# The scan's old state added on VectorE's two diagonal blocks, in place of a unit-matrix product and a mask

## The reference, cut to what matters

```
def step(S, inp):
    r_t, w_t, k_t, v_t, aa_t, bb_t = inp
    sa = jnp.einsum('bhvk,bhk->bhv', S, aa_t)
    S = S * w_t[:, :, None, :] + sa[..., None] * bb_t[:, :, None, :] + v_t[..., None] * k_t[:, :, None, :]
    y_t = jnp.einsum('bhvk,bhk->bhv', S, r_t)
    return S, y_t
```

## Time and profile before

| what | value |
|---|---|
| median of 3 runs | 1130.45 us (1130.41 to 1130.87) |
| profiled execution | 1130.62 us |
| its span in the trace | 1129.0 us |
| PE busy | 1093.8 us (97% of the span) |
| DVE busy | 689.9 us (61%) |
| granted TensorE clock | 0.997 of full speed |

### The profile page before, as it was taken

The page is one execution under the profiler, slowest core; times in us unless marked ns, Lnnn a source line. Parts: engine busy times, 40 slices in busy tenths (PEclk is TensorE's granted clock), DMA queues, the critical chain, the costliest instruction groups (busy, mean ns, idle before and its releaser), DMA issues.

```text
span 1129.0 us, 18123 instructions
## 1 busy us (share of the span) xinstructions
PE 1093.8 (97%) x6736; PEld 862.5 (76%) x6736; DVE 689.9 (61%) x1167; ACT 506.0 (45%) x910; POOL 92.9 (8%) x145
## 2 busy tenths in 40 slices
PE   6999999989999999999999999999999999999996
PEld 5887888767777777777767888888888888888884
DVE  4225566678878777787776444557767677742322
ACT  5436555634533445244543333455565555532222
POOL 8100001101010110101210000100000000000000
PEclk9999999999999999999999999999999999999998
DMA  8632333210111111111323444433333333323321
GB/s 212 129 94 75 93 94 93 75 39 20 39 38 48 56 40 57 48 57 47 104 64 104 140 136 133 130 116 94 93 93 93 93 93 93 89 88 99 89 66 75
DMA packets 171350, 97.00 MB, mean 86 GB/s; under 512 B 30825, under 2 KB 166167, under 8 KB 171287
## 3 DMA queue, kind: packets, MB, share of 16 engines
q1 hardware_dynamic: 165760, 79.72, 25.1%
q0 software_dynamic: 5376, 16.37, 4.7%
q10 hardware_dynamic: 151, 0.04, 0.0%
HBM read 87.71 MB, written 8.39 MB: 85 GB/s over the span
## 4 chain that ended last, share of the span: by engine, by line
PE 88%; DVE 7%; ACT 1%; DMA 1%; issue 1%; SPq 1%; ACTq 0%; DVEq 0%
PE ps L1596 19%; PE ps L1599 19%; PE ps L1598 19%; PE ps L1579 4%; PE ps L1581 4%; PE ps L1580 3%; PE ps L1721 3%; PE ps L1871 2%; PE ps L1850 1%; PE ps L1675 1%; PE ps L1806 1%; PE ps L1669 1%; DMA raw<-in_w_in 1%; DVE wlo L1084 1%; DVE t L1197 1%; PE ps L1783 1%
## 5 line engine op out<-in xcount | busy, mean ns | idle before, releaser
L1084 DVE TENSOR_TENSOR wlo<-raw,whi 128x1024 fp32r<-128x1024 f32 x146 | 178.4, 1222 | 214.5 <-ACT whi L686 214.5
L686 ACT ACTIVATE whi<-raw 128x1024 fp32r<-128x1024 f32 x146 | 154.4, 1057 | 212.3 <-PE ps L1599 204.7
L1596 PE MATMUL ps<-xnh,whi 128*128 128x512 f32 x344 | 136.0, 395 | 0.0
L1598 PE MATMUL ps<-xnl,whi 128*128 128x512 f32 x344 | 135.9, 395 | 0.0
L1599 PE MATMUL ps<-xnh,wlo 128*128 128x512 f32 x344 | 135.9, 395 | 0.0
L1596 PE MATMUL ps<-xh,whi 128*128 128x512 f32 x248 | 99.7, 402 | 1.5 <-DVE xl L1103 1.0
L1599 PE MATMUL ps<-xh,wlo 128*128 128x512 f32 x248 | 97.9, 395 | 0.0
L1598 PE MATMUL ps<-xl,whi 128*128 128x512 f32 x248 | 97.8, 394 | 0.0
L1579 PE MATMUL ps<-xh,whi 128*128 128x512 f32 x184 | 88.5, 481 | 0.0
L1598 PEld LDWEIGHTS ps<-xnl,whi 128*128 128x128 f32 x344 | 64.6, 188 | 15.7
L1599 PEld LDWEIGHTS ps<-xnh,wlo 128*128 128x128 f32 x344 | 64.6, 188 | 15.7
(11 more groups left out here) (323 smaller groups left out, 2152.3 us busy)
## 6 DMA issues: line engine op xcount, KB each, us to landing
raw<-in_w_in SPq DMA_DIRECT2D x108, 256.0 KB, 3.2
raw<-in_w_up SPq DMA_DIRECT2D x88, 256.0 KB, 3.1
raw<-in_w_down SPq DMA_DIRECT2D x32, 256.0 KB, 2.9
gates_scratch<-gst POOLq DMA_DIRECT2D x16, 256.0 KB, 2.4
raw<-in_w_proj_b SPq DMA_DIRECT2D x16, 256.0 KB, 4.0
raw<-in_w_proj_a SPq DMA_DIRECT2D x16, 256.0 KB, 3.0
gl<-gates_scratch POOLq DMA_DIRECT2D x16, 256.0 KB, 3.2
raw<-in_w_out SPq DMA_DIRECT2D x16, 256.0 KB, 3.0
```

Of the source, the lines that this page charges most:

```text
L686: act.activation(flat(whi[:, hb]), flat(raw[:, b]), ACT.Copy).then_inc(w_hi, 1)
L1084: dve.tensor_tensor(flat(wlo[:, hb]), flat(raw[:, b]), flat(whi[:, hb]).bitcast(F32), ALU.subtract).then_inc(w_lo, 1)
L1596: pe.matmul(ps[bank][:, :], whi[:, hb, k, :], hi(k), start=first and k == 0, stop=False)
L1598: pe.matmul(ps[bank][:, :], whi[:, hb, k, :], lo(k), start=False, stop=False)
```

## The change

The unit-matrix product is gone from PE's list. Instead DVE multiplies the old state by the decay into a new tile `decayed` (128x128, all in SBUF), for j = 1 and 2, after `up` and its piece and ahead of the wait for `s_ps`. It waits for that to be written (a new semaphore, `s_decayed`), and then forms the new state with two instructions of 64 partitions by 64 elements, one for each diagonal block: PSUM times the decay plus `decayed`. For j = 0 there is no old state, and the two instructions only multiply. The mask `headones` isn't read there any more; instead POOL clears both buffers of `stm` once at the start (and no longer `zp`, which is written in full each time).

```
-            pool.memset(zp[:, :], 0.0).then_inc(cleared, 1)
+            pool.memset(stm[:, :, :], 0.0).then_inc(cleared, 1)
...
                     if j < NT - 1:
+                        gain = carry[:, d % 2, j + 1:j + 2]
+                        if j:
+                            dve.wait_ge(s_ready, d * (NT - 1) + j)
+                            dve.tensor_scalar(decayed[:, :], stm[:, j % 2, :], gain, None, ALU.mult)\
+                                .then_inc(s_decayed, 1)
+                            dve.wait_ge(s_decayed, d * (NT - 2) + j)
                         dve.wait_ge(s_ps, d * (NT - 1) + j + 1)
-                        dve.scalar_tensor_tensor(stm[:, (j + 1) % 2, :], ps[4 + j % 2][:, 0:P],
-                                                 carry[:, d % 2, j + 1:j + 2], headones[:, :],
-                                                 ALU.mult, ALU.mult).then_inc(s_ready, 1)
+                        for h in range(2):
+                            hs = slice(h * HD, (h + 1) * HD)
+                            dst, src = stm[hs, (j + 1) % 2, hs], ps[4 + j % 2][hs, hs]
+                            if j:
+                                ins = dve.scalar_tensor_tensor(dst, src, gain[hs], decayed[hs, hs],
+                                                               ALU.mult, ALU.add)
+                            else:
+                                ins = dve.tensor_scalar(dst, src, gain[hs], None, ALU.mult)
+                        ins.then_inc(s_ready, 1)
...
                     if j < NT - 1:
-                        if j:
-                            pe.matmul(zb, ident[:, :], stm[:, j % 2, :], start=True, stop=False)
-                        pe.matmul(zb, ktok[:, j, :], vp[:, j, :], start=j == 0, stop=False)
+                        pe.matmul(zb, ktok[:, j, :], vp[:, j, :], start=True, stop=False)
```

More of the change, by code:

```diff
@@ L220, in build @@
         stm = take("stm", [P, 2, P])
+        decayed = take("decayed", [P, P])
         rkones = take("rkones", [P, P])
@@ L347, in build @@
         s_ready = sem("s_ready")
+        s_decayed = sem("s_decayed")
         out_ps = sem("out_ps")
```

## The result

| | before | changed |
|---|---|---|
| median of 5 runs | 1130.45 us (1130.28 to 1130.87) | 1142.12 us (1141.97 to 1142.46) |
| profiled execution | 1130.62 us | 1141.97 us |
| its span | 1129.0 us | 1140.3 us |
| mean granted TensorE clock | 0.997 | 0.990 |

The ratio is 1.0101, 95% interval 1.0089 to 1.0112: 11.7 us slower, where 2.1 us had been forecast and 1136.5 us was the upper end of the range. The page of the changed kernel: span, busy time, and the granted clock in 40 slices of 28.5 us.

The account below looks back on a forecast made before the run. PE is busy 97% of the span, but the scan's PE-DVE relay decides. Removal 0; scans 1 to 6 0.9, scan 0 0.5, scan 7 0.7, total 2.1 us: 1132.6 us (+0.19%), range 1129.8 to 1136.5.

Parts of the forecast that it names:

- The removed product: L1875, 16 times on PE: L1881 still waits for `up`, so the gain is 0.01 us at most, taken as 0.
- The durations: Added DVE instructions without a row: `decayed` 0.28 us, each half of the state 0.285 us.
- the third rival: After `kmod`, POOL's product gets ahead of `decayed` or keeps the halves out: 7.0 us, 1137.5 us; chance 0.10.
- the sum had 0.02: Chunk 2 of scans 1 to 6: state 0.38 us later against 0.35 us of slack, so +0.02 us.
- through `wlo` and `zp` in chunk 0: Scans 1 to 6: the split delays `wlo`, queued behind it, and the already late `zp`: +0.13 us for L1871.
- the second half starts 0.08 us before the first has ended, as everywhere: Split state on DVE: second half starts at 0.20 us, ends at 0.485, 0.13 us later than the single instruction.
- 0.15 was forecast: Delay of each of scans 1 to 6: 0.15 us, six times making 0.9 us.
- 0.5 was forecast for scan 0: Scan 0: 0.13 us in chunks 0 and 1, 0.38 more in chunk 2 without filler; 0.5 us.
- The upper bound of the split (0.27 us): Split state on DVE: each half as long as the full instruction makes 0.62 us, a loss of 0.27.
- I carry the delays to the end without loss: After a scan, engines go on from each other's results, so scan delays pass undiminished to the end; total 2.1 us.
- 0.57 was forecast: Scan 7: 0.13 us through `zp` in chunk 0, and the state 0.44 us later, uncovered, in chunk 1.
- The fourth, a wait or a half dearer than taken: Rival: the same mechanism near its high bounds, 1134 to 1137 us; chance 0.06.

Follow-up runs that it names:

- experiment 5: Changed kernel with the unit-matrix product back on TensorE in chunks 1 and 2 of every scan, its result overwritten: 1141.7 us (1.0095).
- experiment 7: Kernel before with `decayed` computed and waited for in chunks 1 and 2 but read by nothing: 1130.96 us (1.0005).
- experiment 6: Kernel before, unit-matrix product kept, new state written by two 64-partition halves without mask, no `decayed`, POOL clearing `stm`: 1135.03 us (1.0036).
- experiment 1: Changed kernel with both state-writing instructions covering all 128 partitions by 64 columns: 1138.51 us (1.007).
- experiment 8: Changed kernel with the two diagonal blocks written in the other order, partitions 64 to 127 first: 1143.36 us (1.0103).
- experiment 3: Kernel before with scan 7 alone in the new form: 1137.01 us (1.0061).
- experiment 2: Changed kernel with scan 7 in its old form, scans 0 to 6 in the new one: 1134.55 us (1.0048).
- experiment 4: Changed kernel with 14 extra unit-matrix products, never read, in TensorE's waits in scan 7: 1140.02 us (1.0087).
- experiment 9: Changed kernel with a third of a filler k step moved ahead of L1864 in scan 7's chunk 2, another behind the scan: 1140.63 us (1.0072).

## Why the prediction was wrong, step by step

**What held.** The removed product gives nothing: experiment 5 puts it back and scans 2 to 5 keep their length. In the changed kernel `up` ends at 312.58 and L1893 (L1881 before) starts 0.05 behind it, as the prediction said. The durations held too: `decayed` 0.28 us, a half 0.28 to 0.29. `decayed` gets in ahead of POOL's product (313.09 against 313.25), and the halves aren't held off by it, so the third rival is out. `t` took 1.07 us where 1.3 to 1.7 was foretold, but it ended 0.55 us behind POOL's product (314.54 and 315.09), as the prediction reckoned. `decayed` alone costs nothing in scans 2 to 5 (experiment 7); beside the halves it costs about 0.1 us, for a scan loses 0.57 us with it and 0.47 us on average without it (experiment 6), where the sum had 0.02. And most of the loss of a scan, 0.47 us, reaches PE through `wlo` and `zp` in chunk 0, as predicted.

**The term that was mis-sized** is "the second half starts 0.08 us before the first has ended, as everywhere". It doesn't: it starts 0.015 us behind the end, `wlo` starts 0.03 behind the second half and `zp` 0.03 behind `wlo`. The price of the split at `zp` is 0.47 us and not 0.13. Experiments 1, 6 and 8 separate the causes: with all instructions starting at partition 0 the split costs 0.1 us a scan; with the blocks at 0 and 64, 0.41 to 0.49; with the last one at 0 again, 0.24 of the loss comes back. Per scan, 0.57 us was lost where 0.15 was forecast, and 0.92 where 0.5 was forecast for scan 0. The upper bound of the split (0.27 us) didn't hold it either, since it bounded the durations and left the overlap of the neighbours untouched: the case in which an instruction is run alone was on no side of it.

The Trainium skill has this as a model: in "VectorE: DVE Perf Modes", section "Two Vector instructions with no wait between them", an instruction is held until all earlier ones have finished if its input or output starts in another group of 32 partitions than the last input from, or output to, the same memory. By that rule the second half is held, then `wlo` (its SBUF output starts at 0, the half's at 64), then `zp`, the first one to read PSUM since; and with the blocks swapped neither `wlo` nor `zp` is. The timelines of the changed kernel and of experiments 1, 6 and 8 agree with it in each of these places.

**What the sum didn't have at all** is TensorE's clock. "I carry the delays to the end without loss" was the wrong step: 7.1 of the 11.3 us arise behind the start of scan 7. There the second product by `stm` starts 1.02 us later against the scan's first product than before (0.57 was forecast), PE is idle for longer, and it ran at 1.2 GHz for 17 us. Experiment 3 shows that scan 7 alone does it (542.5 us behind its first product against 535.6), experiment 2 that scans 0 to 6 without it leave 535.1, experiments 4 and 9 that with work in the waits scan 7's clock can stay up (536.5 and 536.2, in the one profiled execution of each). So of the 7.1 us about 1 us is delay and about 6 us is the clock. Which part of the form does it is settled in so far as the halves alone didn't (experiment 6) and `decayed` alone didn't (experiment 7), with no run of either below a mean clock of 0.993, and both together did in all six profiled executions that have them in scan 7 without added work: with the unit-matrix product (5) or without, with the blocks in either order (8), and with halves on all partitions (1).

What makes the clock fall in one execution and not in the next stays open. PE's busy time in the scan doesn't tell by itself. In scan 0 the clock stayed up in the changed kernel with 6.49 us of work in 8, and fell in experiment 9 with 6.55 and in experiment 1 with 6.95 in the 8 us up to 265.2. That idle time is the link between the new form and the fall is therefore supported by experiments 4 and 9, and not shown; where the clock fell in their runs at 0.991 is known only for the profiled one of experiment 9. The runs of experiments 4, 8 and 9 fell into kinds 4 to 8 us apart.

**The rivals.** None had the clock. The fourth, a wait or a half dearer than taken (1134 to 1137 us), has the kind of the first part's error. The one closest in size, 1137.5 us through POOL, had another mechanism, and didn't happen. The changed kernel's own 4.2 us before scan 7 would have made it 1134.8 us by the scans alone, and 1135.8 with 1 us of delay in scan 7, inside the range; the clock took it out.

## What to carry to other kernels

Splitting an instruction by partitions cost more here than its second half: the instruction behind it, and the next that read the same memory, stood alone as well. If it has to be split, let the last part start where the neighbours do. And where a serial stretch leaves TensorE partly idle, a delay of a few tenths isn't worth its own length alone: look at the busy share around it and at the granted clock of several executions, and put work into the wait or keep the stretch as it is. Work in the wait was no sure remedy here: six of the nine runs of experiments 4 and 9 still had a mean clock of 0.991, against 0.990 in all five of the changed kernel.

## What the runs showed of the hardware that was not expected

- Two VectorE instructions on partitions 0 to 63 and 64 to 127 take 0.58 us, two of the same width on all partitions 0.48 us. With the order 64, 0 the neighbours overlap by 0.08 us, with 0, 64 they don't.
- In scan 7 TensorE was busy for 5.45 of 8 us and fell to 1.2 GHz, where with 6.7 of 8 it had kept 2.4 GHz. It came back after 17 us (20 us in experiments 5 and 8), though PE was busy for 16.3 of these 17 us. Halves alone, with 6.00 of 8 us, kept it in scan 7 (experiment 6) and lost it in scan 0, where PE had been busy for 6.91 of the 8 us up to 264.7.
- The same program can lose the clock in one run and not in the next: in experiment 9, 1135.2 us at a mean of 0.997 and 1141.8 at 0.991; in the profiled run of the second kind it fell in scan 0. The kernel before never did in its runs here (0.996 to 0.997).
- A VectorE instruction that GpSimd holds up ended at about the same time for two starts: `t` took 1.66 us from 312.08 before and 1.41 us from 312.31 behind `decayed`, and `zp` started at 313.77 and 313.76.
